# Two expert layers, a linear recurrence and two transformer blocks on one core: expert weights streamed as all up tiles and then all down tiles, with the gates' search and spreading placed between the up tiles

## The chip, the core and the metric

The kernel runs on one core of one Trainium2 chip. All weights lie in HBM and are streamed through SBUF once. The time is that of the device for one execution, in microseconds (us); of each kernel the median of several executions is taken. A profiled execution has a time of its own and a span, from its first to its last instruction. The engines are called PE (TensorE), ACT (ScalarE), DVE (VectorE), POOL (GpSimd) and SP (SyncE, which issues the weight loads).

## What is computed

Everything is fp32 on a sequence of 256 tokens of width 1024. The first block has two layers. Layer 0 has an attention with decaying gates, layer 1 a gated linear recurrence; each is followed by a layer of 16,384 small experts, of which each of 8 heads picks 16 for each token:

```python
def peer_ffn(h, w_q, sub_keys, u_tab, v_tab):
    q = (h @ w_q).reshape(B, S, PEER_HEADS, 2, PEER_DQ // 2)
    scores = jnp.einsum('bshpd,hpkd->bshpk', q, sub_keys)
    s1, i1 = lax.top_k(scores[..., 0, :], PEER_TOPK)
    s2, i2 = lax.top_k(scores[..., 1, :], PEER_TOPK)
    cand_s = s1[..., :, None] + s2[..., None, :]          # 16 x 16 candidates
    ...
    top_s, top_pos = lax.top_k(cand_s, PEER_TOPK)
    gate = jax.nn.softmax(top_s, axis=-1)
    ...
        act = jax.nn.gelu(jnp.einsum('thkd,td->thk', u, hx))
        return jnp.einsum('thk,thkd->td', g * act, v_tab[idx])

def rglru_mixer(h, w_in, conv_w, conv_b, w_a, b_a, w_x, b_x, lam, w_out):
    xb, yb = jnp.split(h @ w_in, 2, axis=-1)
    y_gate = jax.nn.gelu(yb)
    xc = depthwise_convolution(xb)
    # per direction: r, ig = sigmoid(block-diagonal linear of xc)
    # log_a = -8 r softplus(-lam);  a = exp(log_a);  mult = sqrt(-expm1(2 log_a))
    # h_t = a_t h_(t-1) + mult * ig * xc
    return ((h_forward + h_backward) * y_gate) @ w_out
```

The second block (two mixers and two convolved feed-forward layers) is the same in both kernels.

## The kernel before

Weights come as tiles of 128 x 1024 fp32 (512 KB), in the order of the table `STREAM`, through a ring of four slots. A token's activations stand as columns: `X`, `H` and the large buffer `BIG` hold chunks of 128 features (or hidden values) by 256 tokens. Each engine runs its own program; semaphores tie them.

There are two ways to multiply by a tile. `linear` (L420) does 8 plain fp32 products with the tile as it came. `split_product` (L426 to L444) does 24 products in fp32r, three for each chunk: for that ACT writes a rounded copy of the tile, `w_high` (`split_high`, L1003), and DVE the difference, `w_low` (`split_low`, L1850), in two halves each. Both buffers hold two tiles, so that `split_high` of tile k waits for the first half of tile k-2 (`mid_tile`) and then for all of it (`tile_done`).

The experts are not gathered: all 16,384 of them are computed for every token, and the gates of those that were not picked are zero. A layer's expert table is 128 up tiles and 128 down tiles; tile j gives hidden values j*128 to j*128+127. Before, the expert layer (`peer`) runs in these stages:

1. 16 query tiles by `linear`; the 32 products with the keys (L585); two copies of the scores out of PSUM (L1129).
2. 36 up tiles ("early") by the plain products of L599, with the gelu of ACT (L1137) into `BIG`. Beside them DVE makes the whole search for both halves of the tokens (`top16`, and the picking of ids).
3. The gates are spread to a dense table, four tokens (a group) at a time, 64 groups: DVE writes for each token a one-hot row of the first key times the gate (L1771) and for all four the one-hot of the second key (L1775); PE multiplies them (L622); ACT copies 92 of the 128 columns to `BIG` (L1166); DVE multiplies the other 36 onto the early hidden values (L1785).
4. 92 up and 92 down tiles, one of each in turn, and then the 36 late down tiles, all by split products. ACT does the gelu (L1184), DVE multiplies by the gates (L1808) and splits the result (`split_gated`, L1857 and L1859).

In layer 1 the recurrence comes before its expert layer: 16 tiles by `linear` (8 for the recurrence's input, then 8 for the gate y), 8 tiles of gate weights (L965) in the order forward reset, forward input, backward reset, backward input, and then on DVE and ACT, one direction after the other, L2217 to L2237; then sum and product (L2240, L2242), and `lru_out` by `linear`.

## Time and profile before

| | |
|---|---|
| median of 3 runs | 3529.12 us (3528.78 to 3529.94) |
| profiled execution, own time | 3533.4 us |
| its span | 3531.7 us |
| PE busy | 3135.8 us (89%) |
| PE weight load busy | 2943.5 us (83%) |
| DVE busy | 2215.4 us (63%) |
| ACT busy | 1331.6 us (38%) |
| mean granted clock of TensorE | 0.947 of full speed |

"Busy" is the time in which an engine has at least one instruction under way. Matmuls overlap, so PE's share says only whether it was fed. In a timeline the distance between the starts of two instructions is what one costs in a row; the duration of one is longer, since it overlaps the next.

### The profile page before, as it was taken

Reading aid. Unit: us, or ns where it says so; the run is one execution under the profiler, and the core shown is the slowest. Engines: PE = TensorE matmul, PEld = TensorE weight load, DVE = VectorE, ACT = ScalarE, POOL = GpSimd, SP = SyncE. Lnnn points to the kernel's source line nnn. Section 1 sums busy time; section 2 is a strip of 40 time slices with the busy share of each in tenths; the row PEclk is TensorE's granted clock in tenths of the full one; section 3 lists DMA queues with packets and bytes.
Section 4 is the critical chain, followed back from the end, with each engine's and each line's share of the span. In section 5 each row is a group of like instructions: output and inputs, shape, how many; then the busy total and the mean of one; then the engine's idle time right before and its main releaser. Section 6 shows DMA issues by size and latency. Waiting matters only on the chain.

```text
span 3531.7 us, 64681 instructions
## 1 busy us (share of the span) xinstructions
PE 3135.8 (89%) x22138; PEld 2943.5 (83%) x22138; DVE 2215.4 (63%) x4652; ACT 1331.6 (38%) x2361; POOL 64.7 (2%) x113
## 2 busy tenths in 40 slices
PE   5977999699999999499869999999897679988898
PEld 4876788599999998388759999999887559987798
DVE  5647168966666674407896666666736327765586
ACT  1110112244444442312224444444452216653374
POOL 2200000000000000000000000000000000000000
PEclk9969999999999999799999999999988779998899
DMA  8930343045555554134205555555430015532353
GB/s 321 410 136 1 104 140 125 0 150 187 186 185 184 185 187 133 66 132 142 83 18 190 185 187 186 185 184 178 157 111 1 21 60 169 174 119 78 120 179 130
DMA packets 137689, 502.47 MB, mean 142 GB/s; under 512 B 15328, under 2 KB 15456, under 8 KB 137344
## 3 DMA queue, kind: packets, MB, share of 16 engines
q1 hardware_dynamic: 122544, 445.63, 37.7%
q0 software_dynamic: 15056, 55.65, 4.1%
q8 instruction: 56, 0.92, 0.1%
q14 instruction: 33, 0.27, 0.0%
HBM read 499.12 MB, written 2.10 MB: 142 GB/s over the span
## 4 chain that ended last, share of the span: by engine, by line
PE 73%; DVE 10%; issue 4%; ACT 3%; DVEq 1%; ACTq 0%
PE PB L420 8%; PE PA L432 8%; PE PA L431 8%; PE PB L430 8%; PE PA L430 8%; PE PB L432 8%; PE PB L431 8%; PE PB L599 7%; DVE onehots L1771 3%; DVE w_low L1850 1%; PE PA L769 1%; PE PB L769 1%; PE PA L965 1%; PE PB L503 1%; DVE onehots L1775 1%
## 5 line engine op out<-in xcount | busy, mean ns | idle before, releaser
L1850 DVE TENSOR_TENSOR w_low<-ring,w_high 128x512 fp32r<-128x512 f32 x1276 | 875.4, 693 | 481.1 <-ACT w_high L1003 473.9
L1003 ACT ACTIVATE w_high<-ring 128x512 fp32r<-128x512 f32 x1276 | 800.3, 632 | 905.9 <-PE PB L432 424.1
L430 PE MATMUL PB<-h_high,w_low 128*128 128x256 f32 x2704 | 772.9, 286 | 30.2 <-DVE h_low L1582 23.0
L432 PE MATMUL PB<-h_high,w_high 128*128 128x256 f32 x2704 | 764.8, 283 | 0.0
L431 PE MATMUL PB<-h_low,w_high 128*128 128x256 f32 x2704 | 764.3, 283 | 0.0
L430 PE MATMUL PA<-a_high,w_low 128*128 128x256 f32 x2400 | 674.7, 281 | 5.2 <-DVE a_low L1859 5.2
L432 PE MATMUL PA<-a_high,w_high 128*128 128x256 f32 x2400 | 675.0, 281 | 0.0
L431 PE MATMUL PA<-a_low,w_high 128*128 128x256 f32 x2400 | 673.1, 280 | 0.0
L430 PEld LDWEIGHTS PB<-h_high,w_low 128*128 128x128 f32 x2704 | 521.2, 193 | 41.9 <-issue 25.8
L431 PEld LDWEIGHTS PB<-h_low,w_high 128*128 128x128 f32 x2704 | 513.9, 190 | 0.5 <-issue 0.5
L432 PEld LDWEIGHTS PB<-h_high,w_high 128*128 128x128 f32 x2704 | 514.3, 190 | 0.0
L430 PEld LDWEIGHTS PA<-a_high,w_low 128*128 128x128 f32 x2400 | 452.6, 189 | 5.8 <-DVE a_low L1859 5.4
L431 PEld LDWEIGHTS PA<-a_low,w_high 128*128 128x128 f32 x2400 | 454.1, 189 | 0.0
L432 PEld LDWEIGHTS PA<-a_high,w_high 128*128 128x128 f32 x2400 | 451.2, 188 | 0.0
L420 PE MATMUL PB<-H,ring 128*128 128x256 f32 x1408 | 312.5, 386 | 17.5 <-ACT H L1088 17.5
L420 PEld LDWEIGHTS PB<-H,ring 128*128 128x128 f32 x1408 | 272.4, 194 | 57.6 <-issue 19.0
L599 PE MATMUL PB<-H,ring 128*128 128x256 f32 x1152 | 252.5, 383 | 7.5 <-ACT BIG L1129 7.5
L599 PEld LDWEIGHTS PB<-H,ring 128*128 128x128 f32 x1152 | 221.1, 192 | 38.5 <-ACT BIG L1129 7.9
L622 PE MATMUL PA<-onehots 128*128 128x128 f32 x1024 | 150.4, 291 | 89.7 <-DVE onehots L1775 86.8
L622 PEld LDWEIGHTS PA<-onehots 128*128 128x128 f32 x1024 | 126.8, 195 | 113.4 <-issue 98.9
L420 PE MATMUL PB<-BIG,ring 128*128 128x256 f32 x512 | 117.3, 393 | 51.6 <-issue 51.2
L420 PEld LDWEIGHTS PB<-BIG,ring 128*128 128x128 f32 x512 | 101.1, 198 | 68.3 <-issue 47.2
(319 smaller groups left out, 3033.6 us busy)
## 6 DMA issues: line engine op xcount, KB each, us to landing
ring<-tiles SPq DMA_DIRECT2D x842, 512.0 KB, 3.3
BIG<-ada POOLq DMA_DIRECT2D x96, 512.0 KB, 14.0
BIG<-skew POOLq DMA_DIRECT2D x4, 512.0 KB, 4.5
X<-x SPq DMA_DIRECT2D x1, 1024.0 KB, 6.1
skew<-BIG POOLq DMA_DIRECT2D x1, 1024.0 KB, 7.0
out<-X SPq DMA_DIRECT2D x4, 256.0 KB, 2.1
con<-consts SPq DMA_DIRECT2D x1, 917.0 KB, 9.2
BIG<-masks POOLq DMA_DIRECT2D x1, 768.0 KB, 6.4
```

Of the source, the lines that this page charges most:

```text
L420: ins = mm(product_slot(q0 + i), wt[:, k * P:(k + 1) * P], src[:, k * T:(k + 1) * T], start=k == 0, stop=k == DC - 1)
L430: mm(dst, lhs_l, high, start=start, stop=False, skip_group_check=True)
L431: mm(dst, lhs_h, low, start=False, stop=False, skip_group_check=True)
L432: return mm(dst, lhs_h, high, start=False, stop=stop, skip_group_check=True)
L503: ins = mm(HEAD_SUMS[0:n, :], c("pick", 12 - h, n), src[:, h * T:(h + 1) * T], start=h == 0, stop=h == n - 1)
L599: ins = mm(PB[:, (i % 4) * 512:(i % 4) * 512 + T], ut[:, k * P:(k + 1) * P], H[:, k * T:(k + 1) * T], start=k == 0, stop=k == DC - 1)
L622: ins = mm(PA[:, (r * 4 + j) * P:(r * 4 + j + 1) * P], onehot_a[:, at:at + P], onehot_b[:, at:at + P], start=True, stop=True)
L769: ins = mm(dst[:, to:to + P], e[lhs][:, at(i)], e[rhs][:, at(i)], start=True, stop=True)
L965: ins = mm(PA[:, (i % 2) * 1024 + j * T:(i % 2) * 1024 + (j + 1) * T], wt[:, (j * 2 + k) * P:(j * 2 + k + 1) * P], LRU["xc"][:, (2 * (m // ...
L1003: fn(tile_half(w_high, s, b), ring[:, at:at + HALF], ACT.Identity).then_inc(sem("high_ready"), 1)
L1771: ts(onehot_a[:, at:at + P], c("iota"), slots[:, bass.ds(tok, 1)], slots[:, bass.ds(tok + 2 * T, 1)], ALU.is_equal, ALU.mult)
L1850: tt(tile_half(w_low, s, b), ring[:, at:at + HALF], tile_half(w_high, s, b).bitcast(F32), ALU.subtract).then_inc(sem("low_ready"), 1)
```

## The change

- All 128 up tiles come first and then all 128 down tiles. Up and down are both split products; the 36 plain early tiles and the zeroing of PSUM (L635) are gone. The hidden values all stay in `BIG`.
- The query tiles are split products too. For that the normalized input goes to `h_high`, `HB` and `h_low` ahead of them.
- A table that is worked out when the program is built (`Plan`) says for each up tile j how many small steps of the search DVE takes beside it (0 to 6, `PLAN.steps`), and which group of tokens is spread behind it (`PLAN.group`). By it, no group stands at j = 0 to 38; groups 0 to 31 stand at two of every three tiles from j = 39 to 85; none at 86 to 91; groups 32 to 63 at every tile from 92 to 123.
- The one-hot rows of the first key are now made by ACT: for each token `Abs(key - iota)` and then `Relu(gate - gate * distance)`, four tokens of a group in the first half, three in the second (DVE makes the fourth). DVE still makes the one-hot of the second key.
- Up tiles whose columns of tokens are spread already (f = `PLAN.folded(j)`) have their gelu in two pieces, and DVE multiplies the first by the gates (`times_gates`); for tiles that are done already when a group is spread, DVE multiplies the group's gates onto them (`fold`).
- Of the 256 sums of two top-16 lists the search looks at 112 only (4 rows of 16, 12 rows of 4), which hold the best 16.
- Recurrence: `lru_in` is cut in `lru_x` ahead of the gate tiles and `lru_y` behind them; the gate tiles come reset first for both directions, then input; each direction has buffers of its own; `exp(2 log_a)` is made by ACT and no longer by a product on DVE; `lru_out` starts when the first pair of chunks is ready.

```diff
+GROUPS = T // 4
+SPLIT_US, TILE_US, GROUP_US = 1.4, 2.86, 0.87
...
+        for j in range(NKEYS):
+            if groups < GROUPS and j >= ready and (groups >= GROUPS // 2 or t == TT or (j - ready) % 3 < 2):
+                self.group[j] = groups
...
+            busy = SPLIT_US + (0.3 if groups else 0) + (1.15 if j in self.group else 0)
+            free += TILE_US + (GROUP_US if j in self.group else 0) - busy - 0.06
...
@@ PE, peer
-                linear(f"wq{layer}", H, chunked=True)
+                split_linear(f"wq{layer}")
...
-                        ins = mm(PB[:, (i % 4) * 512:(i % 4) * 512 + T], ut[:, k * P:(k + 1) * P],
-                                 H[:, k * T:(k + 1) * T], start=k == 0, stop=k == DC - 1)
...
+                def spread_gates(g):
+                    pe.wait_ge(sem("onehot_a_ready"), g0 + g + 1)
+                    pe.wait_ge(sem("onehot_b_ready"), g0 + g + 1)
...
+                for j in range(NKEYS):
+                    if j >= 4:
+                        pe.wait_ge(sem("up_taken"), c0 + j - 3)
+                    split_product(product_slot(j), s0 + j, 0, 8)
+                    if j in PLAN.turned:
+                        turn(PLAN.turned[j])
+                    if j in PLAN.group:
+                        spread_gates(PLAN.group[j])
...
@@ ACT, peer
+                def gelu(j):
+
+                    act.wait_ge(tile_done, r0 + j + 1)
+                    slot, f = product_slot(j), PLAN.folded(j)
+                    if f:
+                        ins = fn(slot[:, 0:f], slot[:, 0:f], ACT.Gelu_apprx_tanh)
+                    if f < T:
+                        ins = fn(BIG[:, j * T + f:(j + 1) * T], slot[:, f:], ACT.Gelu_apprx_tanh)
...
+                    if g0 + g:
+                        act.wait_ge(sem("gates_psum"), g0 + g)
+                    n, done = 3 + (g < GROUPS // 2), sem("key_distance")
...
+                            fn(inv[:, i % 2 * P:(i % 2 + 1) * P], c("iota"), ACT.Abs, scale=-1.0,
+                               bias=slots[:, tok:tok + 1]).then_inc(done, 1)
...
+                            ins = fn(onehot_a[:, i * P:(i + 1) * P], inv[:, i % 2 * P:(i % 2 + 1) * P], ACT.Relu,
+                                     scale=slots[:, 3 * T + tok:3 * T + tok + 1],
+                                     bias=slots[:, 2 * T + tok:2 * T + tok + 1])
...
+                for j in range(NKEYS + 1):
+                    if j:
+                        gelu(j - 1)
+                    if j in PLAN.exp:
+                        act.wait_ge(sem("gate_diff"), w.up(sem("gate_diff")))
+                        fn(piece(PLAN.exp[j], GATE), piece(PLAN.exp[j], GATE), ACT.Exp).then_inc(sem("gate_exp"), 1)
+                    if j - 1 in PLAN.turned:
+                        take_slots(PLAN.turned[j - 1])
+                    if j in PLAN.group:
+                        onehots(PLAN.group[j])
+                    if j - 1 in PLAN.group:
+                        take_gates(PLAN.group[j - 1])
+                    if j < NKEYS:
+                        split_high(run, j + 2)
...
@@ DVE, peer
+                for j in range(NKEYS + 1):
+                    if j and PLAN.folded(j - 1):
+                        times_gates(j - 1)
+                    if j in PLAN.group:
+                        onehots(PLAN.group[j])
+                    if j - 1 in PLAN.group:
+                        fold(PLAN.group[j - 1])
...
+                    if j < NKEYS:
+                        for b in range(2):
+                            for _ in range((PLAN.steps[j] + 1 - b) // 2):
+                                next(choice)
+                            split_low(run, j + 2, halves=(b,))
...
@@ ACT, recurrence
+            for d in range(2):
...
+                fn(a_, la, ACT.Exp).then_inc(sem("lru_a"), 1)
+                gate_branch(3 * d, 3 * d + 1)
+                fn(m_, la, ACT.Tanh, scale=-1.0)
+                fn(la, la, ACT.Exp, scale=2.0).then_inc(sem("lru_squares"), 1)
+                gate_branch(3 * d + 1, 3 * d + 2)
...
+                fn(m_, m_, ACT.Sqrt).then_inc(sem("lru_mult"), 1)
+                gate_branch(3 * d + 2, 3 * d + 3)
...
@@ DVE, recurrence
+            dve.wait_ge(sem("lru_gelu"), w.up(sem("lru_gelu")))
+            dve.wait_ge(taken, product_at["lru_y"][0] + DC)
+            scan(1, 0)
+            scan(1, 1)
```

On PE, at the end of the loop over the groups of layer 0, the program before stands like this (L622 the groups, the last two of the loop's copies; L635 the zeroing, L430 to L432 the first split products; the other rows are the loop's own):

```order
L622 MATMUL PA<-onehots 128x128 x4
L617 REGISTER_ALU
L622 MATMUL PA<-onehots 128x128 x4
L628 REGISTER_ALU
L628 COMPARE_AND_BRANCH
L635 MATMUL PA<-con 128x512 x4
L430 MATMUL PB<-h_high,w_low 128x256
L431 MATMUL PB<-h_low,w_high 128x256
L432 MATMUL PB<-h_high,w_high 128x256
```

Now a group stands behind a split tile, and the next tile behind it; this is the second group, behind up tile 40 of layer 0 (L659 the group, L483 to L485 split products):

```order
L483 MATMUL PB<-h_high,w_low 128x256
L484 MATMUL PB<-h_low,w_high 128x256
L485 MATMUL PB<-h_high,w_high 128x256
L659 MATMUL PA<-onehot_b,onehot_a 128x128 x4
L483 MATMUL PB<-h_high,w_low 128x256
L484 MATMUL PB<-h_low,w_high 128x256
L485 MATMUL PB<-h_high,w_high 128x256
```

The 64 groups no longer stand together: each is between two tiles, and it waits for its one-hots there.

On ACT, the loop over the groups of layer 0 before has one copy for each group and nothing else (L1158 the slots, L1166 the copy):

```order
L1158 ACTIVATE slots<-PA 128x2x3x128
L1170 UNCONDITIONAL_BRANCH
L1170 ISA
L1166 ISA
L1166 ACTIVATE BIG<-PA 128x92x4
L1165 REGISTER_ALU
L1166 ISA
L1166 ACTIVATE BIG<-PA 128x92x4
```

Now, beside up tiles 49 and 50 of layer 0, ACT has the parts of a tile (L1019), the gelu in two pieces (L1166, L1168), the one-hots of a group (L1191 `Abs`, L1196 `Relu`) and the copy of the group before (L1207):

```order
L1019 ACTIVATE w_high<-ring 128x512 x2
L1166 ACTIVATE PB<-PB 128x24
L1168 ACTIVATE BIG<-PB 128x232
L1191 ACTIVATE inv<-con,slots 128x128 x2
L1196 ACTIVATE onehot_a<-inv,slots 128x128 x2
L1191 ACTIVATE inv<-con,slots 128x128 x2
L1196 ACTIVATE onehot_a<-inv,slots 128x128 x2
L1207 ACTIVATE BIG<-PA 128x79x4
L1019 ACTIVATE w_high<-ring 128x512 x2
L1166 ACTIVATE PB<-PB 128x28
L1168 ACTIVATE BIG<-PB 128x228
L1207 ACTIVATE BIG<-PA 128x78x4
```

What moved here is the making of the first key's one-hots, from DVE to ACT, and in front of the weight tile's parts on the same engine.

On ACT, the recurrence before (L1431 the sigmoids of the gates, L1437 `Exp`, L1438 `Tanh`, L1440 `Sqrt`); the copies of y with gelu (L1020) stand ahead of the first row:

```order
L1431 ACT_TABLE_LOAD
L1431 ACTIVATE BIG<-PA,par 128x256 x32
L1437 ACT_TABLE_LOAD
L1437 ACTIVATE BIG<-BIG 128x2048
L1438 ACTIVATE BIG<-BIG 128x2048
L1440 ACT_TABLE_LOAD
L1440 ACTIVATE BIG<-BIG 128x2048
L1437 ACT_TABLE_LOAD
L1437 ACTIVATE BIG<-BIG 128x2048
L1438 ACTIVATE BIG<-BIG 128x2048
L1440 ACT_TABLE_LOAD
L1440 ACTIVATE BIG<-BIG 128x2048
```

And now, up to the second direction's first `Exp` (L1448 the sigmoids, L1464 and L1467 `Exp`, L1466 `Tanh`, L1470 `Sqrt`, L1458 the copies of y):

```order
L1448 ACTIVATE BIG<-PA,par 128x256 x32
L1464 ACT_TABLE_LOAD
L1464 ACTIVATE BIG<-BIG 128x2048
L1458 ACTIVATE BIG<-PB 128x256
L1466 ACTIVATE BIG<-BIG 128x2048
L1467 ACTIVATE BIG<-BIG 128x2048
L1458 ACTIVATE BIG<-PB 128x256
L1470 ACT_TABLE_LOAD
L1470 ACTIVATE BIG<-BIG 128x2048
L1458 ACTIVATE BIG<-PB 128x256
L1464 ACT_TABLE_LOAD
L1464 ACTIVATE BIG<-BIG 128x2048
```

The copies of y moved from ahead of the gates to between the long instructions of the two directions; their gelu stands behind both, for six chunks in one instruction.

## Rows read from the trace of the kernel before

**Rows 1.** Busy time by engine in chosen stretches (the first row names the columns).
```profile
core 0: us, PE busy (x) PEld busy (x) DVE busy (x) ACT busy (x) POOL busy (x), PEclk, DMA share, GB/s
...
599.00:723.00 124.00, 78.29 (x519) 64.80 (x520) 120.70 (x388) 33.34 (x69) 0.00 (x0) 0.99 0.02 5
723.00:1252.00 529.00, 529.00 (x4485) 528.71 (x4484) 349.90 (x656) 260.90 (x465) 0.00 (x0) 1.00 0.56 185
...
1442.00:1488.00 46.00, 0.00 (x0) 0.00 (x0) 36.84 (x42) 17.34 (x13) 0.00 (x0) 0.53 0.03 11
...
3142.00:3223.00 81.00, 80.63 (x652) 75.16 (x650) 48.64 (x103) 49.04 (x121) 0.00 (x0) 1.00 0.43 144
```

**Rows 2.** The chain that ended last: start us, us, what.
```profile
403.07 57.19 PE PB L420 x256
...
471.96 126.27 PE PB L599 x576
...
1347.74 3.73 PE PB L486 x16
...
1355.82 57.19 PE PB L420 x256
1413.47 27.91 PE PA L965 x128
...
1488.18 30.07 PE PB L420 x128
...
2691.76 1.34 PE PB L769 x12
```

**Rows 3.** Timeline, gates being spread: start us, us, engine, what, idle before.
```profile
609.13 1.10 DVE L1771 TENSOR_SCALAR onehots<-con,slots 128x128 f32<-128x128 f32 x4
610.15 0.68 DVE L1775 TENSOR_TENSOR onehots<-con,slots 128x512 f32<-128x512 f32 x1
...
610.75 0.30 DVE L1785 TENSOR_TENSOR BIG<-PA,BIG 128x144 f32 x1
...
610.97 1.15 PE L622 MATMUL PA<-onehots 128*128 128x128 f32 x8 [0.69 <-DVE onehots L1775]
```

**Rows 4.** Timeline, ScalarE: spacing of instructions that stand back to back.
```profile
401.84 4.04 ACT L1088 ACTIVATE H<-H,mod,coef 128x256 f32<-128x256 f32 x8 [2.62 <-DVE H L1576]
...
719.43 2.18 ACT L1003 ACTIVATE w_high<-ring 128x512 fp32r<-128x512 f32 x4
...
2478.12 0.49 ACT L1088 ACTIVATE X<-X,par 128x256 f32<-128x256 f32 x1
2478.52 0.49 ACT L1087 ACTIVATE h_high<-X,par 128x256 fp32r<-128x256 f32 x1
```

**Rows 5.** Groups of ScalarE instructions by shape: x count, busy us, mean ns, idle.
```profile
L1003 ACT ACTIVATE w_high<-ring 128x512 fp32r<-128x512 f32 x1276 | 800.3, 632 | 905.9 <-PE PB L432 424.1 <-PE PA L432 424.0 <-DMA ring<-tiles 35.7
L1184 ACT ACTIVATE act_v<-PB 128x256 f32<-128x256 f32 x184 | 67.2, 365 | 0.0
...
L1088 ACT ACTIVATE H<-H,mod,coef 128x256 f32<-128x256 f32 x32 | 16.2, 587 | 10.5 <-DVE H L1576 10.5
...
L1155 ACT ACTIVATE BIG<-BIG 128x128 f32<-128x128 f32 x4 | 1.2, 309 | 9.9 <-DVE BIG L1753 9.9
```

**Rows 6.** Timeline, VectorE: low parts of two weight tiles, back to back.
```profile
720.15 2.50 DVE L1850 TENSOR_TENSOR w_low<-ring,w_high 128x512 fp32r<-128x512 f32 x4 [0.28 <-ACT w_high L1003]
```

**Rows 7.** Timeline of the recurrence's first direction.
```profile
1447.11 1.89 ACT L1438 ACTIVATE BIG<-BIG 128x2048 f32<-128x2048 f32 x1
1449.02 1.28 ACT L1440 ACT_TABLE_LOAD   x1
...
1453.76 1.91 ACT L1440 ACTIVATE BIG<-BIG 128x2048 f32<-128x2048 f32 x1 [3.45 <-DVE BIG L2225]
...
1458.41 4.77 DVE L2237 TENSOR_TENSOR_SCAN BIG<-BIG 128x256 f32<-128x256 f32 x8
...
1485.68 2.29 DVE L2242 TENSOR_TENSOR BIG<-BIG 128x2048 f32<-128x2048 f32 x1
```

More of the change, by code:

```diff
@@ L111 @@
+PLAN = Plan()
 class Tally:
@@ L667, in conv_ffn @@
+                down(0)
+                steps = (NKEYS - 2) // 4
+                with pe.Fori(0, steps) as it:
+                    for j in range(1, 5):
+                        down(j, it)
+                for j in range(4 * steps + 1, NKEYS):
+                    down(j)
             def conv_ffn(i):
@@ L1065, in rms @@
                     squares(two(X, i), two(SQUARES, i), "squares_ready")
+                    if run is not None and i == 1:
+                        split_high(run, 0)
                 root(name)
+                if run is not None:
+                    split_high(run, 1)
             def layer_norm(name, run=None):
@@ L1161, in peer @@
-                g0 = layer * 64
-                gates = chunks(BIG[:, :])
-                def group(r, it):
-                    act.wait_ge(sem("gates_psum"), it * 4 + (g0 + r + 1))
-                    fn(gates[:, 0:MAIN, bass.ds(it * 16 + r * 4, 4)],
-                       PA[:, r * 512:(r + 1) * 512].rearrange("p (t j) -> p j t", t=4)[:, 0:MAIN, :],
-                       ACT.Identity).then_inc(sem("gates_copied"), 1)
-                with act.Fori(0, 16) as it:
-                    for r in range(4):
-                        group(r, it)
@@ L1195, in peer @@
[L1195 to L1207 removed]
+                act.wait_ge(sem("first_scores"), layer + 1)
@@ L1822, in peer @@
+            def peer(layer):
+                run, c0, g0 = f"experts{layer}", layer * NKEYS, layer * GROUPS
+                r0 = STREAM_AT[run][0]
+                spans(dve, lambda k, it: split_low(f"wq{layer}", k, it, 4), (2, 2 * PEER_HEADS))
                 split_low(run, 0)
                 split_low(run, 1)
-                split_low(run, 2)
-                gated(0)
-                split_low(run, 3)
-                gated(1)
-                steps = (MAIN - 2) // 4
-                with dve.Fori(0, steps) as it:
-                    for j in range(2, 6):
-                        column(j, it)
@@ L1844, in split_low, with onehots @@
-            def split_low(run, k, it=0, step=8):
+                gates = chunks(BIG[:, :])
+                multiplied = sum(PLAN.folded(j) > 0 for j in range(NKEYS))
+                def onehots(g):
+                    if g % (GROUPS // 2) == 0:
+                        dve.wait_ge(sem("slots_ready"), w.up(sem("slots_ready")))
+                    if g0 + g:
+                        dve.wait_ge(sem("gates_psum"), g0 + g)
+                    if g >= GROUPS // 2:
+                        tok = 4 * g + 3
+                        ts(onehot_a[:, 3 * P:], c("iota"), slots[:, tok:tok + 1], slots[:, 2 * T + tok:2 * T + tok + 1],
+                           ALU.is_equal, ALU.mult)
+                    column = slots[:, T + 4 * g:T + 4 * g + 4]
+                    tt(chunks(onehot_b[:, :], P), over(c("iota"), 4), wide(column.unsqueeze(2), P, 4, P),
+                       ALU.is_equal).then_inc(sem("onehot_b_ready"), 1)
@@ L1846, in split_low, with late @@
+                def late(j, it):
+                    split_low(run, NKEYS + j, it, 4)
+                    split_gated(c0 + j, BIG[:, bass.ds(it * (4 * T) + j * T, T)], r0 + NKEYS + j - 2, it)
+                dve.wait_ge(sem("up_taken"), c0 + NKEYS)
+                spans(dve, late, (2, NKEYS))
+                add_sums(run, modulation(layer, 1, 2))
+            def split_low(run, k, it=0, step=8, halves=(0, 1)):
                 n, s = STREAM_AT[run][0] + k, SPLIT_AT[run][0] + k
-                for b in range(2):
+                for b in halves:
```

687 lines of the change are left out of this document (340 added, 347 removed).

## Prediction

> **What bounds the kernel now.** I read the busy time by stretch first, then the chain that ended last, then timelines of the places that the change touches. In the split stage PE is the bound: 4485 products in 529 us, 0.118 us each, 24 for a tile, so 2.831 us a tile, with PE busy all the time at full clock while DVE and ACT are busy for 350 and 261 us of it [rows 1]. The plain tiles take longer: 57.19 us for 16 query tiles (3.57), 126.27 us for 36 early tiles (3.51) [rows 2]. The gates' stage (599 to 723) is DVE's: DVE is busy for 120.7 of 124 us, PE for 78 [rows 1]; a group takes 1.84 us (609.13 to 610.97), all of it DVE's own instructions [rows 3]. In the recurrence (1442 to 1488) PE does nothing and its granted clock falls to 0.53 [rows 1]. So three kinds of places run above PE's split rate: plain tiles by some 0.7 us each (52 in a layer), the gates' stage, where 124 us hold 64 groups of four products (57 us at 0.89 a group, below), and the 46 us of the recurrence.
>
> **The change part by part**, in layer 0's times; layer 1 has the same stages with the same durations.
>
> *Query tiles.* The plain ones end at 403.07 + 57.19 = 460.26 [rows 2]. Split ones need, for each pair of chunks, four ACT instructions instead of two, at the spacing of (4.04 - 0.59)/7 = 0.49 us [rows 4, 5]. They start at 401.84, so the 16 end at 409.7; DVE's difference adds 0.7, the last six products of the first tile 0.7: 411.2. Fifteen tiles at 2.831 follow: 453.7, a gain of 6.6 us. The parts of these tiles (ACT 1.04, DVE 1.21 us a tile, below) hide behind 2.83.
>
> *Keys.* Before, 11.7 us from 460.26 to the first early product at 471.96 [rows 2]. Now the first half's scores are copied while PE makes the second half's: 0.5 for the last query copy, 32 products at 1.34/6 = 0.223 us [rows 2], 7.2, and one copy, 1.9 by the slope of ACT below, with 0.2 of waits: 9.8. Up tile 0 starts at 463.5.
>
> *Up tiles without groups.* 45 of them before the last group (j = 0 to 38, 86 to 91) and four after it, at 2.831: 138.7 us. Their cover: DVE has 1.21 us of low parts ((2.50 - 0.69)/3 = 0.60 for a half [rows 6]) and, by the plan's free time (2.86 - 1.4 - 0.06 in the diff), 1.40 us of search; ACT has 1.04 and a gelu of 0.3. If DVE needed over 2.83 it would pace them (rival 3). Turning the slots costs PE 0.9 us twice.
>
> *What ACT needs for a group.* It has no row for `Abs` or `Relu` on 128 x 128, so I build it. Slope: (632 - 309)/384 = 0.84 ns a column [rows 5]. Spacing for 256 columns: 0.40 with one per-partition operand, 0.49 with two [rows 4]; less 128 columns, 0.29 for `Abs` and 0.39 for `Relu`. Four tokens: 2.72 us. Bounds: without any such operand 0.19 each, so 1.5; with no overlap 0.39 and 0.48, so 3.5. I take 2.72, since the spacings are of the same engine, SBUF to SBUF, with the same kinds of operands. A weight part is (2.18 - 0.63)/3 = 0.52 [rows 4], the gelu in two pieces 0.35 (0.365 less 0.1 of overlap, plus a second start [rows 5]).
>
> *Groups 0 to 31* stand at two of three tiles, a, b and c. PE alone needs 3 x 2.831 + 2 x 0.89 (four products) = 10.28 us. But the one-hots can be begun only when the tile before has ended, since the weight part and the gelu ahead of them in ACT's queue wait for it. From the end of c: wait 0.13, part 0.65, gelu 1.00, one-hots 3.72, seen by PE at 3.87. Tile a ended at 2.83, so PE waits 1.04; the group ends at 4.76, tile b at 7.59. ACT goes on: two parts 4.76, gelu 5.11, one-hots 7.83, seen at 7.98; PE waits 0.39, group 8.87, tile c 11.70. By then ACT has copied both groups out and is level with PE. DVE's sum in the cycle is low parts 3.6, `times_gates` 0.7, second-key one-hots 1.2, folds 0.6 (spacings as in [rows 3]), search 2.7 (by the plan's formula), and 1.8 of waiting for ACT's copy in b: 10.6, below 11.7. So 11.70 a cycle: 15 cycles and 8.87, 184.4 us, against 161.6 if PE paced. The second `Exp` of the softmax falls on j = 73, where ACT has no slack: 0.3 and two table loads of 1.28 [rows 7], 2.9 us. The first, at j = 26, has slack.
>
> *Groups 32 to 63* stand at every tile. PE needs 3.72; ACT 0.52 + 0.35 + 2.04 for three tokens + 0.17 (the last `Relu` waits for its `Abs`) + 0.14 + 0.52 = 3.74. One-hots are seen 3.35 after the last tile's end, in time. DVE: low parts 1.2, one one-hot 0.26, the four 0.6, times 0.3, fold up to 0.6: 3.0. So 32 x 3.74 and 0.5 at the first: 120.2.
>
> Up tiles in all: 138.7 + 1.8 + 184.4 + 2.9 + 120.2 = 448.0. Down: 128 x 2.831 = 362.4; the casts and differences are as in the late tiles of before, which run inside the 2.831. End: 463.5 + 448.0 + 362.4 = 1273.9 for the last product; with the 1.8 us of adds and squares that stand there now too, 1275.7 for the mean of squares, which was at 1347.74 [rows 2]. Gain 72 us a layer, 144 in both.
>
> *Recurrence* (times from its first product, 1355.82 [rows 2]). Eight x tiles end at 29.5, eight gate tiles 27.9 later at 57.4, and the eight y tiles then run on PE beside the scans, off the path. The reset gates of both directions come first, so DVE has made both log_a and one of the two gated inputs ahead of 57.4. The last sigmoids end at 59.0; then ACT: load 1.3, three long instructions 1.8 apart and a copy, 66.1; DVE 2.3, ACT's `Sqrt` 1.9, DVE 2.3, eight scans 4.8 [rows 7]: 77.6. The second direction's three long ones are done at 77.9; DVE 80.3, `Sqrt` 82.3, product 84.6. The gelu of y (load 1.3, six chunks 1.5, two more copies) is done at 86.2, and the second direction's scans wait for it. Four scans, a sum and a product of a pair: `lru_out` starts at 90.1, instead of 1488.18 - 1355.82 = 132.4. Its first tile is then paced by pairs, 3.8 us lost; the 30.07 us of before held some 2 at a low clock (27.9 for eight warm tiles [rows 2]), of which I give back 1.4. Gain 42.3 - 3.8 + 1.4 = 40.
>
> Sum: 3533.4 (the profiled execution's own time) - 144 - 40 = 3349; the median lay 4.3 below that execution, so **3345 us**.
>
> A table load is 1.28 us here and starts 0.02 after the `Tanh` ahead of it ended (1449.00, 1449.02), so it costs its own length and the lost overlap [rows 7]. The Trainium skill (ScalarE: Activation LUTs, What ACT_TABLE_LOAD costs) has 1.38 us of draining on top of each switch, 2.66 in all. By that rule the nine switches on the path (two in each layer's cycle, five in the recurrence) would cost 12 us more: an estimate of 3357.
>
> **The rivals.**
>
> 1. *PE paces the groups too* (13%). If ACT's short instructions overlap more than by my rows, the one-hots are there in time: 26.5 us less a layer, 3292. It needs the four tokens in 1.6 us, near the lower bound. For it: no row shows two such short instructions in a row. Against: the spacings of rows 4.
> 2. *ACT's short instructions do not overlap at all* (15%), since every `Relu` waits for an `Abs`. At 3.5 us for four tokens the same walk gives a cycle of 13.3 and, for three tokens, 4.3 a tile: 44 us more a layer, 3432.
> 3. *DVE paces tiles 0 to 38* (17%): the plan fills it to 2.8 of 2.86 us, each list of the search ends in a wait for its own results, and a part that stands alone takes 0.69 instead of 0.60. At 0.3 over, that is 12 us a layer, and some 6 more in the cycles: 3380.
> 4. *PE's instruction supply* (4%), the slower side. Both up phases are written out, 128 tiles of 24 products and 24 weight loads, where loops stood. If the supply added 0.72 us to each of 256 up tiles, all 184 us were gone, and beyond that the kernel is slower than 3529. Against it: 24 tiles of the last mixer are written out too and 652 products take 81 us there, with other work between [rows 1]; but 24 tiles are few.
>
> My forecast has 48%; 3% is left for others.
>
> **How the numbers follow.** 3345 is the likeliest case. The range 3290 to 3420 takes in rival 1, rival 3 and most of the way to rival 2, for which 3432 is the extreme, and leaves out about 2 in 10. Within 0.2% (7 us) of 3529 a measurement can't tell from no change. Faster: 94%; same: 2%; slower: 4%, from rival 4.
>
> **What would show it.** Up tiles 0 to 38 in 110 us; PE waiting for ACT's `onehot_a` by about 1.0 and 0.4 us in each three tiles up to j = 85, and hardly from 93 on; the four pairs of `Abs` and `Relu` in 2.7 us; down tiles at 2.83; `lru_out` 90 us after `lru_x` began. The prediction is wrong if PE waits for `w_low` in the tiles without groups (DVE paces), if the pairs take 3.5 us or 1.6, or if PE waits for nothing that shows between its own instructions in the written-out phase.

## The result, and the profile after

The changed kernel takes 3356.39 us in the median of 4 runs (3354.36 to 3357.36), the kernel before 3529.53 in 4 runs beside it (3528.78 to 3535.06): a ratio of 0.9505, with an interval of 0.9489 to 0.9522. The forecast was 3345, in a range of 3290 to 3420. The profiled execution took 3355.62 us, with a span of 3353.6 against 3531.7 before.

The page's busy time, and three of its costliest groups:

```profile
PE 3045.9 (91%) x22954; PEld 2911.2 (87%) x22954; DVE 2192.1 (65%) x4518; ACT 1719.0 (51%) x3655; POOL 64.7 (2%) x113
...
L1196 ACT ACTIVATE onehot_a<-inv,slots 128x128 f32<-128x128 f32 x448 | 198.6, 485 | 2.1
L659 PE MATMUL PA<-onehot_b,onehot_a 128*128 128x128 f32 x1024 | 141.7, 282 | 38.5 <-ACT onehot_a L1196 34.9
...
L1191 ACT ACTIVATE inv<-con,slots 128x128 f32<-128x128 f32 x448 | 156.3, 391 | 0.0
```

`Relu` (L1196) takes 0.485 us and `Abs` (L1191) 0.391, as taken from the rows of the affine instructions [rows 4]. PE waits 38.5 us ahead of the gates' products, 34.9 of them for ACT's `onehot_a`.

The chain that ended last gives the stages (start us, us, what; the rows answer to [rows 2]):

```profile
395.58 1.76 DVE inv L1607
...
452.54 3.84 PE PA L635 x32
...
461.92 0.39 PE PB L483
...
1274.58 3.73 PE PB L539 x16
...
1282.66 30.61 PE PB L473 x128
1313.27 27.64 PE PA L982 x128
...
1405.42 3.47 PE PA L539 x16
...
2288.51 3.74 PE PB L539 x16
```

From the reciprocal ahead of the query tiles to the mean of squares behind the experts it is 1274.58 - 395.58 = 879.0 us (before 1347.74 - 399.32 = 948.4), and 879.1 in layer 1 (2288.51 less 1409.42): 69.4 us gained in each. The recurrence, mean of squares to reciprocal, went from 174.6 (1347.74 to 1522.32) to 134.8 (1274.58 to 1409.42): 39.7. The part ahead of layer 0's query tiles is 3.7 shorter, the part behind layer 1's experts 4.3 longer. 2 x 69.4 + 39.7 + 3.7 - 4.3 = 177.9 of the 178.1 by which the spans differ.

The last two terms belong to nothing that was changed. Over the 13 changed kernels of this study the first reciprocal started between 395.3 and 399.5 us, and the part behind layer 1's experts, from its reciprocal on, took 1053.6 to 1062.9 (1060.8 here, 1056.5 before), with the same instructions. So differences of medians below some 5 us are not read here; the stages of one trace against another are, with care. The expert stage of the changed kernel's own code stands in six layers of three traces (the changed kernel, unsorted, y_first): five took 878.9 to 879.1 us, the sixth (y_first, layer 1) 875.7, because more of it ran at full clock. The recurrence took 133.3 to 135.1 us for the same code.

Layer 0's experts by stretch: tiles 0 to 38, groups 0 to 31, tiles 86 to 127 with groups 32 to 63, down tiles.

```profile
core 0: us, PE busy (x) PEld busy (x) DVE busy (x) ACT busy (x) POOL busy (x), PEclk, DMA share, GB/s
461.90:574.70 112.80, 112.78 (x944) 112.78 (x945) 99.83 (x324) 63.73 (x122) 0.00 (x0) 0.98 0.56 187
574.70:762.80 188.10, 169.25 (x1382) 162.77 (x1380) 134.54 (x413) 166.87 (x477) 0.00 (x0) 1.00 0.41 134
762.80:911.20 148.40, 147.97 (x1271) 147.77 (x1271) 115.68 (x236) 134.02 (x393) 0.00 (x0) 1.00 0.45 147
911.20:1274.60 363.40, 361.77 (x3073) 361.56 (x3071) 256.61 (x511) 161.02 (x255) 0.00 (x0) 1.00 0.56 185
```

PE paces three of the four stretches. In the second it is busy for 169 of 188 us and ACT for 167: neither is full, since they wait for each other. One cycle of tiles a, b and c there:

```profile
586.09 0.63 ACT L1019 ACTIVATE w_high<-ring 128x512 fp32r<-128x512 f32 x1 [0.72 <-PE PB L485]
586.62 0.16 ACT L1166 ACTIVATE PB<-PB 128x8 f32<-128x8 f32 x1
586.68 0.40 ACT L1168 ACTIVATE BIG<-PB 128x248 f32<-128x248 f32 x1
586.98 0.68 ACT L1191 ACTIVATE inv<-con,slots 128x128 f32<-128x128 f32 x2
587.56 0.87 ACT L1196 ACTIVATE onehot_a<-inv,slots 128x128 f32<-128x128 f32 x2
588.33 0.68 ACT L1191 ACTIVATE inv<-con,slots 128x128 f32<-128x128 f32 x2
588.91 0.87 ACT L1196 ACTIVATE onehot_a<-inv,slots 128x128 f32<-128x128 f32 x2
...
589.84 1.16 PE L659 MATMUL PA<-onehot_b,onehot_a 128*128 128x128 f32 x8 [0.96 <-ACT onehot_a L1196]
```

Four one-hots take 589.68 - 586.98 = 2.70 us on ACT (the next instruction starts at 589.68); they start only behind the gelu of the tile that has just ended, and PE, through with tile a, has stood 0.96 us. The next a group starts at 601.71: a cycle of 11.87.

### The profile page after: what moved, and what is told of

It is laid out like the page before. It is cut to its first block, busy times and chain, and to the rows that moved or that the text cites. A ratio compares the mean times of both kernels' runs of the same rounds, so it can differ in the third digit from the quotient of the medians.

```text
span 3353.6 us, 65287 instructions
## 1 busy us (share of the span) xinstructions
PE 3045.9 (91%) x22954; PEld 2911.2 (87%) x22954; DVE 2192.1 (65%) x4518; ACT 1719.0 (51%) x3655; POOL 64.7 (2%) x113
## 4 chain that ended last, share of the span: by engine, by line
PE 69%; ACT 11%; DVE 7%; issue 2%; DVEq 1%; ACTq 0%
PE PB L483 9%; PE PB L485 9%; PE PB L484 9%; PE PA L485 9%; PE PA L483 8%; PE PA L484 8%; PE PB L473 4%; PE PA L659 3%; ACT onehot_a L1196 3%; ACT inv L1191 2%; ACT w_high L1019 2%; DVE w_low L1928 1%; PE PA L785 1%; PE PB L785 1%; DVE BIG L1954 1%
## 5 line engine op out<-in xcount | busy, mean ns | idle before, releaser
L1019 ACT ACTIVATE w_high<-ring 128x512 fp32r<-128x512 f32 x1484 | 915.1, 629 | 883.8 <-PE PA L485 472.3
L483 PE MATMUL PB<-h_high,w_low 128*128 128x256 f32 x3536 | 1023.2, 289 | 48.6 <-DVE h_low L1616 36.5
L485 PE MATMUL PB<-h_high,w_high 128*128 128x256 f32 x3536 | 1003.2, 284 | 0.0
L484 PE MATMUL PB<-h_low,w_high 128*128 128x256 f32 x3536 | 1003.0, 284 | 0.0
L483 PEld LDWEIGHTS PB<-h_high,w_low 128*128 128x128 f32 x3536 | 685.6, 194 | 64.2 <-issue 39.4
L483 PE MATMUL PA<-a_high,w_low 128*128 128x256 f32 x2400 | 676.9, 282 | 5.0 <-DVE a_low L1937 5.0
L485 PE MATMUL PA<-a_high,w_high 128*128 128x256 f32 x2400 | 676.7, 282 | 0.0
L485 PEld LDWEIGHTS PB<-h_high,w_high 128*128 128x128 f32 x3536 | 675.5, 191 | 0.0
L484 PEld LDWEIGHTS PB<-h_low,w_high 128*128 128x128 f32 x3536 | 675.4, 191 | 0.0
L483 PEld LDWEIGHTS PA<-a_high,w_low 128*128 128x128 f32 x2400 | 453.7, 189 | 5.4 <-DVE a_low L1937 5.4
L485 PEld LDWEIGHTS PA<-a_high,w_high 128*128 128x128 f32 x2400 | 452.3, 188 | 0.0
L473 PE MATMUL PB<-H,ring 128*128 128x256 f32 x896 | 198.5, 385 | 8.8 <-ACT H L1108 8.8
L473 PEld LDWEIGHTS PB<-H,ring 128*128 128x128 f32 x896 | 173.6, 194 | 33.5 <-issue 9.5
L1196 ACT ACTIVATE onehot_a<-inv,slots 128x128 f32<-128x128 f32 x448 | 198.6, 485 | 2.1
L659 PE MATMUL PA<-onehot_b,onehot_a 128*128 128x128 f32 x1024 | 141.7, 282 | 38.5 <-ACT onehot_a L1196 34.9
L659 PEld LDWEIGHTS PA<-onehot_b,onehot_a 128*128 128x128 f32 x1024 | 124.5, 191 | 51.9 <-ACT onehot_a L1196 51.9
L1191 ACT ACTIVATE inv<-con,slots 128x128 f32<-128x128 f32 x448 | 156.3, 391 | 0.0
```

Of the source, the lines that this page charges most:

```text
L473: ins = mm(product_slot(q0 + i), wt[:, k * P:(k + 1) * P], src[:, k * T:(k + 1) * T], start=k == 0, stop=k == DC - 1)
L483: mm(dst, lhs_l, high, start=start, stop=False, skip_group_check=True)
L484: mm(dst, lhs_h, low, start=False, stop=False, skip_group_check=True)
L485: return mm(dst, lhs_h, high, start=False, stop=stop, skip_group_check=True)
L659: ins = mm(PA[:, (g % 4 * 4 + i) * P:(g % 4 * 4 + i + 1) * P], onehot_a[:, i * P:(i + 1) * P], onehot_b[:, i * P:(i + 1) * P], start=True, ...
L1019: fn(tile_half(w_high, s, b), ring[:, at:at + HALF], ACT.Identity).then_inc(sem("high_ready"), 1)
```

## Experiments

All are edits of the changed kernel; their ratios are to the kernel before, timed beside them.

| run | median us | ratio, interval |
|---|---|---|
| changed kernel | 3356.39 | 0.9505, 0.9489 to 0.9522 |
| act3 | 3321.81 | 0.9406, 0.9387 to 0.9424 |
| early | 3407.07 | 0.9643, 0.9626 to 0.9660 |
| act3_early | 3358.76 | 0.9510, 0.9491 to 0.9528 |
| dve_all | 3323.15 | 0.9407, 0.9389 to 0.9426 |
| plain_wq | 3369.30 | 0.9542, 0.9526 to 0.9558 |
| warm | 3358.85 | 0.9513, 0.9498 to 0.9528 |
| unsorted | 3357.03 | 0.9511, 0.9492 to 0.9531 |
| y_first | 3387.81 | 0.9596, 0.9578 to 0.9614 |
| act2 | 3303.60 | 0.9360, 0.9346 to 0.9373 |
| early2 | 3353.14 | 0.9495, 0.9480 to 0.9510 |
| act3_early2 | 3329.67 | 0.9429, 0.9415 to 0.9444 |
| act2_warm2 | 3315.51 | 0.9395, 0.9380 to 0.9410 |

### Who paces groups 0 to 31: act3, dve_all, act2

```diff
-                    n, done = 3 + (g < GROUPS // 2), sem("key_distance")
+                    n, done = 3, sem("key_distance")
...
-                    if g >= GROUPS // 2:
+                    if True:
                         tok = 4 * g + 3
                         ts(onehot_a[:, 3 * P:], c("iota"), ...
```

> The fourth one-hot of groups 0 to 31 is made by DVE too, as in groups 32 to 63; ACT makes three. Theory (ACT paces the cycle of three tiles, 11.87 us measured): the walk of the prediction with 2.2 us of one-hots instead of 2.72 leaves one wait of about 0.5 us before the a group and none in b, a cycle of 10.8 to 10.9, so 15 us less in a layer: about 3326 us. Rival (DVE has no room there; with the search its sum for a cycle was 10.6 and becomes 11.1, waits for ACT's copies in it): the cycle stays at 11.3 or more and PE begins to wait for w_low, 3340 to 3356. If ACT did not pace at all, 3356.

The a groups stand 10.95 us apart (588.89, 599.84, 610.79), and the median is 34.6 us lower. By stages it is 15.0 us in layer 0 (864.0 for 879.0). DVE took the fourth one-hot at no price.

In dve_all, ACT's `onehots` is gone and DVE makes `for i in range(4)`.

> DVE makes all first-key one-hots in both halves (four instructions is_equal and mult at about 0.26 us), ACT none: the one-hots' place before the change, in the new order. Theory (ACT's one-hots cost 1.3 us a cycle in groups 0 to 31, but DVE can't take them all): DVE's sum is 10.6 + 2.1 less the 1.8 of waits that ACT's earlier copies free, 11 to 12.7 a cycle, and in groups 32 to 63 DVE needs 3.0 + 0.8 = 3.8 against 3.72: between 13 us less and 20 more a layer, I take 5 more, 3366 us. Rival (DVE has far more room than its listed busy time says): near act3, 3330.

It was the rival: the median is 3323.15, the cycle 10.9. That is also the low end of my sum (10.6 + 2.1 - 1.8); the 5 us more that I took had left part of DVE's waits for ACT in its work. In 167 us of this phase (578 to 745) DVE is busy for 120.45 in the changed kernel, and with all one-hots for 160.74, 96%: there it has no room left.

act2 gives each engine two:

```diff
-                    n, done = 3 + (g < GROUPS // 2), sem("key_distance")
+                    n, done = 2, sem("key_distance")
...
+                    for i in (2, 3):
+                        tok = 4 * g + i
+                        ts(onehot_a[:, i * P:(i + 1) * P], c("iota"), slots[:, tok:tok + 1],
+                           slots[:, 2 * T + tok:2 * T + tok + 1], ALU.is_equal, ALU.mult)
```

> ACT makes the first two first-key one-hots of every group, DVE the other two. Theory: with three the cycle came to 10.95 us, one-hots late by about 0.6 before a; with two, ACT is through 2.5 us and DVE about 2.5 us after the last tile's end (1.0 to the gelu, one product, two one-hots, the four of the second key), both before tile a's end at 2.83, so PE paces: 10.3 to 10.4 a cycle, 9 us less in a layer than with three, 3304 us. Rival (something else holds the a group at 10.9, since with all four on DVE it was 10.9 too): 3320.

3303.60 us, the fastest kernel here: 52.8 less than the changed kernel. Its a groups stand 10.37 apart (587.75, 598.11, 608.48), and its expert stages take 854.8 and 854.9 us instead of 879.0 and 879.1. So the edit is worth 48.4; most of the rest is the unchanged last part, which at 1053.6 us was the shortest of all. The waits, in the changed kernel from 574.7 to 762.8 us (engine, line, waited for, us in total, times, longest):

```profile
DVE BIG L1892 <- ACT BIG L1207: 26.7, 16, 3.4
DVE w_low L1928 <- ACT w_high L1019: 25.7, 19, 1.9
PEld PA L659 <- ACT onehot_a L1196: 25.3, 32, 1.9
ACT w_high L1019 <- PE PB L485: 21.9, 30, 0.9
PE PA L659 <- ACT onehot_a L1196: 17.0, 17, 1.7
```

and in act2 from 574.7 to 739.5, the same tiles:

```profile
ACT w_high L1019 <- PE PB L485: 34.6, 45, 1.1
DVE w_low L1926 <- ACT w_high L1019: 8.8, 19, 0.8
...
PE PA L659 <- ACT onehot_a L1196: 0.2, 1, 0.2
```

Now ACT waits for PE and no longer PE for ACT; DVE's waits for ACT, 52 us, have shrunk to some 10. The phase is 23.3 us shorter (188.1 less 164.8), nearly all of the layer's 24.2, and PE is busy for 163.95 us of it.

### Amount of work or place in the queue: early, act3_early, early2, act3_early2

`ahead(j)` is true for tiles of kind a. In early and act3_early their one-hots stand one tile earlier, behind the cast (`split_high`):

```diff
+                    if j in PLAN.group and not ahead(j):
                         onehots(PLAN.group[j])
...
                     if j < NKEYS:
                         split_high(run, j + 2)
+                    if ahead(j + 1):
+                        onehots(PLAN.group[j + 1])
```

> All four one-hots stay with ACT, but those of group a are queued one tile earlier, behind tile c's cast (c has no group), so they can't be late for a. Theory (it is the place in ACT's queue, behind the last tile's gelu, that makes PE wait 0.96 us before a, not ACT's amount of work): the wait before a goes, the one before b (0.33) stays or grows since ACT's own sum for a cycle is 10.7 to 10.9: cycle 10.7 to 10.9, about 15 us less in a layer, 3326 us. Rival (ACT's throughput paces and its real sum is near 11.9, short instructions overlapping less than I took): no gain, 3350 to 3356, the wait only moves to b.

> Both edits together. Theory: ACT has then 9.4 us of work in a cycle in which PE has 10.28, and the one-hots are there in time, so PE paces: cycle 10.3 to 10.4, about 24 us less in a layer than 11.87, 3308 us. Rival (DVE paces at 11 us or more with the search, one more one-hot and the waits for copies): 3330 to 3345, with PE waiting for w_low or onehot_b between tiles 39 and 85.

Both expectations fell: 50.7 us slower than the changed kernel, and 37 slower than act3. In early's trace, at tile c (ACT, DVE and PE):

```profile
628.45 0.68 ACT L1191 ACTIVATE inv<-con,slots 128x128 f32<-128x128 f32 x2
...
630.39 0.86 ACT L1196 ACTIVATE onehot_a<-inv,slots 128x128 f32<-128x128 f32 x2
631.16 0.17 ACT L1166 ACTIVATE PB<-PB 128x32 f32<-128x32 f32 x1
631.24 0.37 ACT L1168 ACTIVATE BIG<-PB 128x224 f32<-128x224 f32 x1
...
631.64 0.19 DVE L1890 TENSOR_TENSOR BIG<-PB,BIG 128x32 f32<-128x32 f32 x1 [2.38 <-ACT BIG L1168]
631.75 0.68 DVE L1883 TENSOR_TENSOR onehot_b<-con,slots 128x512 f32<-128x512 f32 x1
...
632.54 1.56 PE L659 MATMUL PA<-onehot_b,onehot_a 128*128 128x128 f32 x8 [1.84 <-issue]
```

The cast's second half waits for the end of tile c, so the one-hots behind it start hardly earlier than before, and now c's gelu stands behind them. DVE's `times_gates` waits for that gelu, and `onehot_b` stands behind `times_gates`. PE waits 1.84 us, for DVE (`onehot_b` is done at 632.43). The a groups are 13.9 apart (618.66, 632.54).

Only about half of early's loss is this wait. Behind it the granted clock falls in 12 of the 15 cycles of each layer, and 7 to 17 products of tile b stand 0.21 apart instead of 0.118: group b then comes 5.3 us after group a, and 4.05 where the clock holds. Two cycles of early, one of each kind:

```profile
618.66:632.54 13.88, 12.04 (x89) 11.87 (x89) 8.25 (x25) 10.72 (x31) 0.00 (x0) 0.88 0.33 114
660.39:673.11 12.72, 10.77 (x89) 10.40 (x89) 8.52 (x25) 10.53 (x32) 0.00 (x0) 1.00 0.37 125
```

At full clock a cycle takes 12.7, 0.9 more than in the changed kernel, so some 13 of the 26.3 us by which layer 0's stage is longer are the wait and some 14 (12 x 1.15) the clock. act3_early has the wait alone: its cycles of 12.04 (591.20, 603.24) are at full clock, 1.1 more than act3's.

In early2 and act3_early2 the two lines stand ahead of the cast:

```diff
+                    if ahead(j + 1):
+                        onehots(PLAN.group[j + 1])
                     if j < NKEYS:
                         split_high(run, j + 2)
```

> The earlier queueing of group a's four one-hots on ACT again, now ahead of tile c's cast instead of behind it; behind the cast they stood ahead of c's gelu, for which DVE's onehot_b waits, and the cycle was 13.9. Theory: the one-hots are then made during tile c and only ACT's own sum for a cycle (two groups of 2.75, two copies of 0.55, three tiles of 1.45) is left, 10.95 us: 14 us less in a layer than 11.87, 3328 us. Rival (any work put ahead of c's gelu makes onehot_b late again): 12 or more a cycle, 3360 or more.

> Three one-hots on ACT, one on DVE, and group a's queued during tile c ahead of its cast. Theory: nothing but PE paces, 10.3 to 10.4 a cycle, 3304 us, the same as with two on each engine. Rival (work ahead of c's gelu makes onehot_b late): 11.5 to 12 a cycle, 3340 to 3355.

Neither came as expected. early2 has the changed kernel's time, within what medians can tell, and most of its cycles take 11.7 to 11.9; act3_early2 is 8 us slower than act3 by medians and 1.8 in layer 0's stage, with cycles of 11.1. The one-hots are made earlier, but c's casts behind them are late; DVE's low part waits for them (early2: from 646.8 to 648.39), and `onehot_b` is behind the low parts:

```profile
647.73 1.14 ACT L1019 ACTIVATE w_high<-ring 128x512 fp32r<-128x512 f32 x2
...
648.39 0.69 DVE L1933 TENSOR_TENSOR w_low<-ring,w_high 128x512 fp32r<-128x512 f32 x1 [1.61 <-ACT w_high L1019]
...
650.24 0.68 DVE L1883 TENSOR_TENSOR onehot_b<-con,slots 128x512 f32<-128x512 f32 x1
...
651.02 1.13 PE L659 MATMUL PA<-onehot_b,onehot_a 128*128 128x128 f32 x8 [1.03 <-issue]
```

So what has to be done between a tile's end and its group paces this phase, by ACT with four one-hots (11.87) and with three (10.95), and by DVE when it makes all four (10.9); with two on each PE paces (10.37). Neither of the two places tried got round it: what is moved ahead of the gelu or the cast comes back through DVE.

### The query tiles and their clock: plain_wq, warm, act2_warm2

plain_wq takes `wq0` and `wq1` out of the split runs:

```diff
-                split_linear(f"wq{layer}")
+                linear(f"wq{layer}", HB, sem("whole_ready"))
...
-                split_evacuate(f"wq{layer}", 0)
+                evacuate(f"wq{layer}", big(0, 2 * PEER_HEADS * T))
```

> The 16 query tiles of each layer are plain fp32 products again (no casts, no differences of weights; the halves of h are still made for the up tiles), all else as in the changed kernel. Theory A (what the traces show from the reciprocal to the keys, 60.9 us before and 57.0 after, holds by itself): 4.0 us a layer more, 3364 us. Theory B (the prediction's term, 6.6 a layer, was right and something else ate 2.6 of it): 13 us more, 3369.

12.9 us more, by the number theory B. But the run is a poor judge between them: reciprocal to the first product with the keys takes 64.08 us (399.54 to 463.62), where the kernel before took 61.5 (399.32 to 460.81) and the changed one takes 56.96. (The 60.9 in theory A ends with the last query product, not with the keys.) The 2.6 us over the kernel before fit ACT's second instruction for each chunk of h, which this run keeps. So undoing it this way costs 7.1 a layer in this stretch, and the change itself gained 4.5, not 6.6: 2.1 are missing, not 2.6.

For where they went, the changed kernel's first query tiles: up to 410.7 us PE's products are 0.21 apart instead of 0.118, and the granted clock is 0.50 (1.2 GHz). warm puts work into the wait ahead of them:

```diff
             def peer(layer):
+                for _ in range(13):
+                    mm(PA[:, 1024:1024 + T], ident, c("pairs", 0, T), start=True, stop=True)
                 split_linear(f"wq{layer}")
```

> PE gets 13 extra plain products (5.7 us at full clock) into an unused bank of PA in the 6.0 us in which it waits for h_low ahead of each layer's query tiles; their result is used by nobody. Theory (the 2.6 us that the query tiles lost against the prediction is the half clock at which the first 48 products run after that idle time): the products ahead keep the clock, the first tile is paced by ACT's pairs alone, 2.5 us less a layer, 3351 us. Rival (the first tile is held by ACT's pairs anyway and the rest is something else): within 1 us of the changed kernel, 3356.

The median shows no gain. The windows of warm, ahead of, in and behind the first tile (PEclk is the granted clock):

```profile
398.00:404.00 6.00, 5.80 (x27) 4.75 (x26) 4.89 (x6) 4.26 (x9) 0.00 (x0) 1.00 0.22 80
404.00:410.00 6.00, 2.85 (x18) 2.29 (x18) 2.17 (x5) 5.75 (x12) 0.00 (x0) 1.00 0.00 0
410.00:414.00 4.00, 4.00 (x21) 4.00 (x21) 2.44 (x4) 0.94 (x3) 0.00 (x0) 0.57 0.40 127
```

The extra products did hold the clock at 1.00, but in the first tile, paced by ACT's pairs, PE is busy for 2.85 of 6 us, and behind it the clock falls: the half-speed stretch is put off: its last part was 406.9 to 410.7 us, now it is 410.0 to 413.5. Reciprocal to keys is 56.65 us in layer 0 and 55.92 in layer 1, 0.3 and 1.0 less than in the changed kernel, not 2.5.

The whole expert stages are 1.9 and 2.6 us shorter all the same (877.10 and 876.49), too little for a median to show. The other 1.6 in each is up tile 0: in the changed kernel its first 17 products run at half clock, here at full clock. They did so too in layer 0 of plain_wq and layer 1 of y_first, without extra products, so what decides it stays open.

act2_warm2 also fills the three waits inside the tile:

```diff
+                        if fresh is not None and m in (2, 4, 6) and k in (wq0, wq1):
+                            for _ in range(2):
+                                mm(PA[:, 1024:1024 + T], ident, c("pairs", 0, T), start=True, stop=True)
```

> Two one-hots on ACT and two on DVE as in the run before, and PE kept busy ahead of and inside the first query tile: 13 plain products into an unused bank ahead of it and two more (0.87 us) ahead of each of its three later waits for h_low (0.94 to 1.08 us each). With the 13 alone the granted clock was 1.0 up to 408 us and fell at 410 us, after the waits in that tile. Theory: with the waits filled too the second tile runs at full clock, 2 us less in a layer than act2: 3300 us. Rival (the waits don't matter for the clock): as act2, within 1 us, or slower by what the extra products delay.

11.9 us slower than act2, for a reason that neither expectation had. The 16 tiles run in a loop of four tiles, and the fill stands in the first of them: the trace has 48 of its products (L497) in layer 0, 12 in each of tiles 0, 4, 8 and 12. The 36 behind tile 0 cost 36 x 0.218 = 7.85 us. In the first tile the clock holds:

```profile
401.00:407.00 6.00, 5.68 (x34) 4.33 (x32) 2.59 (x4) 5.28 (x11) 0.00 (x0) 1.00 0.00 0
407.00:412.00 5.00, 5.00 (x45) 5.00 (x44) 3.30 (x6) 2.64 (x6) 0.00 (x0) 1.00 0.55 174
```

The clock stays at 1.00 throughout. Reciprocal to keys takes 62.92 us (395.27 to 458.19); less 7.85 it is 55.07, 1.9 below the 56.96 of the changed kernel and of act2, and the same in layer 1. In layer 0 of the ten kernels with split query tiles and no fill it is 56.9 to 57.0. In layer 1 it is 55.1 to 57.0, and the 55.12 of y_first came without a fill, though the granted clock was 0.70 over most of its first tile:

```profile
1442.00:1448.00 6.00, 4.31 (x19) 3.57 (x19) 2.23 (x4) 5.65 (x12) 0.00 (x0) 0.70 0.00 0
```

So the fill gains 1.9 us where the clock would have stayed low to the tile's end. With it in tile 0 alone, act2 would take up to 4 us less than 3303.6; that is worked out, no run shows it.

### The recurrence: unsorted, y_first

```diff
-                kind, d, half = i // 4, (i // 2) % 2, i % 2
+                d, kind, half = i // 4, (i // 2) % 2, i % 2
...
-    put("lru_gates", g.transpose(1, 0, 2, 5, 3, 6, 4, 7).reshape(8, P, TILE))
+    put("lru_gates", g.transpose(0, 1, 2, 5, 3, 6, 4, 7).reshape(8, P, TILE))
```

> Only the order of the recurrence's gate tiles is undone (direction first, then kind; DVE scales and multiplies in that order). Theory: with both in the trace ahead of the last sigmoids, all that remains behind the last gate tile is one product (2.3 us of DVE, beside ACT's table load and three long instructions, 7 us), so the order is worth nothing: 3355 to 3358. Rival (log_a of the second direction must be early, and the gated product late is on the path): 2 to 5 us more, 3360.

The recurrence takes 134.8 us (1276.44 to 1411.28), as in the changed kernel: the theory. Sorting the gates by kind brought nothing.

y_first streams `lru_y` ahead of `lru_gates`, ACT copying it at once:

```diff
-    ("lru_x", DC), ("lru_gates", 8), ("lru_y", DC), ("lru_out", DC),
+    ("lru_x", DC), ("lru_y", DC), ("lru_gates", 8), ("lru_out", DC),
```

> The recurrence's eight y tiles stand ahead of the gate tiles again (ACT copies them at once and does their gelu in one piece at its old place in the end), all else as in the changed kernel. Theory (most of the 39.7 us is y's tiles, which now run beside the scans): 27.9 us more, less about 1 for ACT's copies that leave the chain: 3383 us. Rival (the gain is mostly the earlier log_a and paired scans, and y's tiles delay something behind ACT where they stand now): 10 to 18 us more, 3366 to 3374.

The stage takes 161.75 us (1274.89 to 1436.64), 26.9 more than 134.8: the theory's 27.9 less 1. The median is 31.4 higher, but the four executions spread from 3383.31 to 3393.05; the profiled one, the lowest, is 27.7 above that of the changed kernel. x and y form one block ahead of the gates:

```profile
1282.98 58.25 PE PB L473 x256
1341.23 27.64 PE PA L983 x128
```

So of the recurrence's 39.7 us, 26.9 are y's tiles beside the scans, none is the order of the gate tiles, and the remaining 12.8 belong to the rest of the edit (both directions' scaled gates and gated inputs ready ahead of the last sigmoids, squares by `Exp` on ACT, gelu in one piece, sums and products by pairs), which I did not take apart.

## Why the prediction was right, and where it was off

**The mechanism.** What bounds each stretch came as forecast: PE without groups, in groups 32 to 63 and in the down tiles; in groups 0 to 31 PE and ACT alternately. The forecast was 11.3 us too low: by medians the gain is 173, not 184, and by spans 178. Of the 6 in the spans, 2 x 2.6 are the layers (69.4 for 72), 0.3 the recurrence, and 0.5 the unchanged parts (3.7 less 4.3). The other 5 are spread between executions: I had taken 4.3 off, because the median of before lay that far below its profiled execution, and the changed kernel's median is 0.8 above its own. The 2.6 of a layer is itself a sum in which errors cancel: 2.1 too little for the query tiles and 1.3 for the up tiles (1.5 in tiles 0 to 38, 0.8 in groups 0 to 31, 1.0 too much behind them), and 0.8 too much for the down tiles. That it comes so near is partly luck; the terms one by one are what bears the forecast out.

**Query tiles: the term that was mis-sized.** I had 54.4 us from the reciprocal to the end of the last query tile (399.32 to 453.7); measured are 56.5 (395.58 to 452.1, where its copy starts), a gain of 4.5 for the 6.6 forecast. The clock was left out: for the kernel before I read the granted clock of the recurrence [rows 1], but for the new first tile I took full-speed products, though PE stands 6 us ahead of it. The fill in act2_warm2 gives 1.9 of the 2.1 back.

**Keys.** 9.8 forecast, 9.8 measured (452.1 to 461.92).

**Up tiles.** Tiles 0 to 38 took 112.8 us for the 110 forecast and 0.9 for a turn. The first 17 products ran at half clock (0.21 apart from 461.92 to 465.6), which cost 1.6 us; the turn took 1.0. They are 2.826 us apart otherwise, so rival 3 is out, with DVE busy for 99.83 of 112.8. Rival 4 is out too: in 128 written-out tiles PE waits for nothing but the named engines, being busy for 112.78 of 112.8 us in the first stretch and 147.97 of 148.4 in the third.

**Groups 0 to 31.** Forecast were a cycle of 11.70 and waits of 1.04 and 0.39, 1.43 in all; measured is 11.87, with PE idle for 0.96 ahead of a and 0.1 ahead of b. Idle time leaves out the overlap that a wait also costs, so the sum is better read against act2, where PE never waits: 10.37 for the cycle (10.28 forecast), so the waits cost 1.50. Group b starts 4.11 behind group a, and 3.82 in act3 without a wait: 0.3 of it, and 1.2 is ahead of a. The four one-hots take 2.70, for 2.72 forecast. Rival 1 needed 1.6 and rival 2 3.5. Their prices hold up in the experiments all the same: when PE paces, in act2, the layer is 24.2 us shorter, for 26.5 in rival 1.

**The softmax's second `Exp`.** Forecast 2.9, measured 5.73 - 4.11 = 1.62 between the groups around it. The second table load and the copy beside it fall into tile c, where ACT has slack; I had charged both.

```profile
709.96 1.28 ACT L1216 ACT_TABLE_LOAD   x1
711.26 0.31 ACT L1216 ACTIVATE BIG<-BIG 128x128 f32<-128x128 f32 x1
711.47 0.68 ACT L1191 ACTIVATE inv<-con,slots 128x128 f32<-128x128 f32 x2
```

**Table loads.** Here a load starts as soon as the gelu ahead of it has ended (709.65 + 0.30) and takes 1.28 us, as in [rows 7]. The Trainium skill (ScalarE: Activation LUTs, What ACT_TABLE_LOAD costs) has 1.38 us of draining on top, and by it the time would have been 3357: that is near the measured 3356, but no switch in this trace shows the extra time: in the two Exp switches of layer 0 the next instruction starts 0.01 us after the load. The 11 us lie elsewhere, as above. Of the nine switches that I had put on the path, the one back to the gelu stands where ACT has slack, and the two ahead of a `Sqrt` end 0.9 us before DVE's product is ready.

**Groups 32 to 63.** Forecast 120.2, measured 32 x 3.713 and 0.4 at the first. I had put ACT 0.02 above PE's own rate; PE paced.

**Down tiles.** 363.4 us with the last squares (911.2 to 1274.58), 364.2 forecast.

**Recurrence.** The walk from `lru_x` to the start of `lru_out` gave 90.1 us; it was 1373.30 - 1282.66 = 90.6. The order of the gate tiles, by which I had both log_a ready early, had no share in it (unsorted).

## What to carry to other kernels

Where three engines pass work round, sum what an engine must do between one engine's end and the next one's start, not its busy share: ACT was busy for 89% of the groups' phase and PE for 90%, and halving what stood between them (four one-hots on ACT to two, the other two on DVE) gave 48.4 us, while queueing the same work earlier gave nothing or cost up to 50, because it stood ahead of something a third engine waited for. Half of those 50 was PE's clock, which fell behind the longer waits: price a wait with what follows it. In a sum of an engine's load keep its waits for the others apart: with them in, DVE looked full at 10.6 of 11.7 us, and it could take every one-hot at a cycle of 10.9. A stretch in which PE is fed in pieces, or stood still just before, is to be priced at the clock that the neighbouring rows show.
